# Tile products of a blockwise inverse in two PSUM banks, and other slots for the small work around them, in a gated DeltaNet and S5 decoder step

## The chip, the cores and the metric

One Trainium2 chip, one core. The metric is the device time of one execution of the whole program, in microseconds. In the profile PE is TensorE's matmuls, PEld its weight loads, DVE VectorE, ACT ScalarE, POOL GpSimd, SP the engine that only issues DMAs.

## The reference, cut to what matters

The program is one inference step of a two-layer decoder trunk on 1024 prompt tokens and 8 sample tokens, model width 1024. Layer 0 mixes tokens with a gated DeltaNet, layer 1 with an S5 state-space mixer; each is followed by a SwiGLU FFN. The change touches the DeltaNet mixer alone:

```
qkv, z, b, a = split(h @ w_in);  qkv = silu(short_conv(qkv));  q, k = l2norm(q), l2norm(k)
kb   = k * beta;   decay = exp(gc_i - gc_j) below the diagonal       # gc: running sum of g in a chunk
lmat = tril(kb @ k.T * decay, -1)
w, u = (I + lmat)^-1 @ [kb * exp(gc), v * beta]                      # the inverse, chunk by chunk
per chunk:  v_new = u - w @ S;  o = (q * exp(gc)) @ S + (q @ k.T * decay) @ v_new
            S = S * exp(g_last) + k_dec.T @ v_new
out = (rmsnorm(o) * silu(z)) @ w_out
```

There are 8 query/key heads, each with two value heads. All of it is float32.

## The kernel before, in words

**Staging.** The kernel works on transposed activations, [feature, token], 1032 tokens in three blocks of 344. It goes through a prologue, the mixer, FFN, S5 mixer, GLU and a second FFN. A weight matrix goes through the array as a high and a low part (whi, wlo), so that one product takes three matmuls. POOL makes the two parts of the next weight unit as soon as PE has finished the unit that held the buffer (`split`, L2099 to L2102: a cast, then a subtraction).

**The mixer** loops over 8 head pairs i (`HQK`). A pair has first its dense part: six units of projection (`dense_steps`, L626), with convolution, silu and norms on ACT and DVE. Then come four quads q. A quad is two chunks of 128 tokens of two heads, so four 128 x 128 matrices to invert. The inverse is built by levels: four levels of 32 x 32 tile products along the diagonal (`levels`, `tiles`, L660), a fifth (L762, L767, L773) and a sixth of 64 x 64 (L783, L789). Each level is the same exchange: PE makes the product P of the stored factor (NM) with the inverse so far; ACT copies P out of PSUM (PP, L1020); PE makes the products T and Y from it; DVE adds both to TY (L1282). Nothing of the next level can start before that.

**What fills the waits.** A quad has 12 slots, two to a level, and every engine's program is written out by hand in that order (`slot` in each of `mix_pe`, `mix_act`, `mix_dve`). In a slot stand pieces of other work: steps of the recurrence of the quad before (`chain`, L671, L677, L683 to L690: kS, vn, o, S); pieces of the output projection of the pair before (`out_piece`, L702, six matmuls each, in the slots that `PIECE_SLOTS` names, added into x by `add_x`, L1172); the gate's norm (`gate_sq`, the matmul with ones L638, `gate_r`, `gate_mul` L1085 and L1086, `gate_hi` L883, `gate_lo` L1092); the next quad's Gram product (L653, slot 7) and what DVE makes of it (`triangle` L1124 and L1128 in slot 8, `first_y` L1134 to L1139 in slot 9, which the next quad's first level waits for); the samples' small products (L727, slot 5).

**At a quad's end**, ACT has in slot 9 `spread_t` (two copies, L900), `diagonal` (three copies of the next quad's diagonal blocks, L894), `spread_y` (four copies, L905), and in slot 10 `fifth_y` (two copies, L911) and the copy of VB (L962). DVE has the copy T5 (L1285). PE's sixth level (L783) waits for T5 and Y5; its second product (L789) waits for ACT's copy PP6 (L1022); DVE copies the result to Y (L1288), and the next quad's vn waits for that.

**Banks.** PSUM has eight banks. The tile products of matrix j use bank j (`LEV`, banks 0 to 3), with P, T and Y in separate columns; the recurrence has bank 4. So the fillers of a quad (`aside`) have banks 5, 6 and 7, and take the one that is free first by the slot number given to it. A bank taken again is waited for until its reader is done. The dense part takes seven banks in turn (`take`). The bank of the Gram product is given as free one slot on, while its reader (`triangle`) runs in slot 8.

Of the kernel before, what the change touches and what calls it, by code (L numbers as in the profile page):

```python
# [23 lines left out]
P = 128  # L24
# [29 lines left out]
def build(nc, dr, plan):  # L54
    ctx = ExitStack()
    with ctx:
# [502 lines left out]
        COL_P, COL_T, COL_Y = 0, Z, 2 * Z  # L559
        DENSE = (0, 1, 2, 3, 5, 6, 7)  # L560
        LEV, CB = (0, 1, 2, 3), 4
# [4 lines left out]
        def across(col, w, r=slice(0, P)):  # L566
            return ps[r, 0:4, col:col + w]
        PIECE_SLOTS = ((0, 1, 2, 3, 4, 7, 8, 9), (0, 2, 3, 4, 6, 7), (0, 3, 4, 7, 8), (0, 3, 4, 6, 7))
# [25 lines left out]
        def mix_pe(p):  # L594
            held = {}
            dense = 0
            free = {5: 0, 6: 0, 7: 0}
# [8 lines left out]
            def take(who, name):  # L606
                nonlocal dense
                dense += 1
                return use(DENSE[(dense - 1) % 7], who, name)
# [46 lines left out]
            def tiles(col, lhsT, rhs):  # L656
                for d in range(4):
                    for j in range(4):
                        r = zone((j + d) % 4)
                        ins = nc.tensor.matmul(ps[r, LEV[j], col:col + Z], lhsT(r, j), rhs(r, j), start=True, stop=True)  # L660
                return ins

            def chain(i, q, k):
# [9 lines left out]
                elif k % 4 == 1:  # L673
                    p.after("DVE", g + "Y6")
                    b = use(CB, "ACT", g + f"vn{c}")
# [77 lines left out]
            def fifth_level(i, q):  # L753
# [4 lines left out]
                for j in range(4):  # L758
                    for h in range(2):
                        jj = (j + h) % 4  # L760
                        up, low = zone(2 * h), zone(2 * h + 1)
                        ins = nc.tensor.matmul(ps[low, LEV[jj], COL_P:COL_P + Z], DEC[q % 2][up, jj, low], W[up, jj, 0:Z], start=True, stop=True)  # L762
# [3 lines left out]
                for j in range(4):  # L766
                    ins = nc.tensor.matmul(ps[zone(1), LEV[j], COL_T:COL_T + Z], W[zone(1), j, Z:2 * Z], PP[zone(1), j], start=True, stop=True)  # L767
                p.go(ins, gq + "T5")
                for j in range(4):
                    for h in range(2):  # L770
                        jj = (j + h) % 4
                        up, low = zone(2 * h), zone(2 * h + 1)
                        ins = nc.tensor.matmul(ps[up, LEV[jj], COL_Y:COL_Y + Z], PP[low, jj], W[low, jj, Z:2 * Z], start=True, stop=True)  # L773
                p.go(ins, gq + "PY5")

            def last_level(i, q):
# [3 lines left out]
                p.after("DVE", gq + "T5")  # L780
                p.after("ACT", gq + "Y5")
                for j in range(4):
                    ins = nc.tensor.matmul(ps[H:P, LEV[0], j * H:(j + 1) * H], DEC[q % 2][0:H, j, H:P], TOP[0:H, j], start=True, stop=True)  # L783
# [1451 lines left out]
```

How the kernel before makes its waits and increments, by code:

```python
            def until(self, who, value):  # L126
                if value > self.seen.get(who, 0):
                    self.e.wait_ge(sems[who], value)
                    self.seen[who] = value
# [73 lines left out]
        def wait_weights(p, u):  # L203
            p.e.wait_ge(w_split, place[u] + 1)
            return place[u] % 2
# [124 lines left out]
        def norm_blocks_dve(v, gi, ready=None):  # L330
            V = nc.vector
            for n in range(2):
                for kt in range(KT):
                    if square_by(n, kt) == "DVE":
                        square(v, n, kt, ready)
            v.e.wait_ge(in_par, 16 * 6)
            for k in range(NC3 * KT + 2):
                n, kt = divmod(k, KT)
                if n < NC3:
                    if k >= RING:
                        v.after("DVE", f"lo{(k - RING) // KT}.{(k - RING) % KT}")
                    v.after("ACT", f"rms{n}")
                    v.go(V.scalar_tensor_tensor(ring(nh, k), x[:, kt, blk(n)], gains[:, gi, kt:kt + 1], nr[:, blk(n)], ALU.mult, ALU.mult), f"h{n}.{kt}")
                if k >= 2:
                    n, kt = divmod(k - 2, KT)
                    v.after("ACT", f"hi{n}.{kt}")
                    v.go(V.tensor_tensor(hlo[:, kt, blk(n)], ring(nh, k - 2), hhi[:, kt, blk(n)].bitcast(F32), ALU.subtract), f"lo{n}.{kt}")
# [64 lines left out]
        def pro_pe(p):  # L412
            p.e.wait_ge(const_ready, 1)
            def low_bank(who, name):
                plan[("bank", p.pfx + name)] = int(name[-1])
                return int(name[-1])
```

## Time and profile before

| what | value |
|---|---|
| three runs, median | 3659.48 us (3659.13 to 3660.59) |
| the profiled execution, its own time | 3668.19 us |
| its span, first to last instruction | 3666.5 us |
| busy: PE, PEld, DVE, ACT, POOL | 3337.3, 3143.0, 1865.3, 827.3, 847.5 us |
| granted TensorE clock, mean | 0.922 |
| DMA | 223.82 MB, mean 61 GB/s |

The profiled execution took 8.7 us more than the median run. A granted clock of 1.00 is 2.4 GHz, 0.50 is 1.2 GHz; a mean between them is a mixture of stretches at these two.

### The profile page before, as it was taken

What the parts mean: (1) busy time and instruction counts of PE and PEld (TensorE: products, weight loads), DVE (VectorE), ACT (ScalarE), POOL (GpSimd) and SP (SyncE); (2) the same over time, 40 slices, a digit from 0 to 9 for tenths busy, and PEclk for the clock granted to TensorE, in tenths of its full rate; (3) what the DMA queues carried; (4) which work ended last, traced back from release to release, by engine and by line L of the source; (5) the groups of instructions that cost most, each with busy time, mean ns of one, the idle gap of its engine ahead of it and who ended that gap; (6) DMA issues with size and microseconds to landing.
All of it is one profiled execution on the core that took longest, in us unless ns stands there. A gap on an engine that the chain in (4) does not pass through costs nothing.

```text
span 3666.5 us, 74612 instructions
## 1 busy us (share of the span) xinstructions
PE 3337.3 (91%) x32699; PEld 3143.0 (86%) x32699; DVE 1865.3 (51%) x4027; ACT 827.3 (23%) x1897; POOL 847.5 (23%) x776
## 2 busy tenths in 40 slices
PE   6889898989898898988999999995699899999998
PEld 5878797978787787877999999994499799999997
DVE  5445555455554454556876777635512433423334
ACT  3334333324242332333010111002200300000001
POOL 2102020202020111201333333332323133333331
PEclk8879898989898897989999999996699899999999
DMA  2111111111111111110112222226611011111111
GB/s 90 55 42 50 59 44 59 47 49 52 48 54 44 55 55 49 48 42 30 49 61 84 72 84 78 71 65 217 180 41 47 29 47 47 47 47 47 47 48 62
DMA packets 111348, 223.82 MB, mean 61 GB/s; under 512 B 24880, under 2 KB 59184, under 8 KB 110000
## 3 DMA queue, kind: packets, MB, share of 16 engines
q1 hardware_dynamic: 82400, 177.66, 15.2%
q10 hardware_dynamic: 28624, 41.38, 3.5%
q8 instruction: 259, 4.24, 0.5%
q14 instruction: 65, 0.53, 0.1%
HBM read 177.86 MB, written 41.14 MB: 60 GB/s over the span
## 4 chain that ended last, share of the span: by engine, by line
PE 85%; DVE 8%; ACT 3%; issue 2%; DMA 2%; SPq 1%; POOL 0%; POOLq 0%; DVEq 0%; ACTq 0%
PE ps L218 31%; PE ps L626 15%; PE ps L1360 14%; PE ps L702 5%; PE ps L660 4%; PE ps L677 1%; PE ps L234 1%; PE ps L671 1%; PE ps L653 1%; PE ps L638 1%; DVE x L1172 1%; PE ps L727 1%; PE ps L789 1%; PE ps L295 1%; DVE dwork L1282 1%
## 5 line engine op out<-in xcount | busy, mean ns | idle before, releaser
L218 PE MATMUL ps<-hhi,whi 128*128 128x344 f32 x2424 | 779.1, 321 | 19.1 <-DVE hlo L1829 15.3
L218 PE MATMUL ps<-hhi,wlo 128*128 128x344 f32 x2424 | 776.3, 320 | 0.0
L218 PE MATMUL ps<-hlo,whi 128*128 128x344 f32 x2424 | 775.6, 320 | 0.0
L2099 POOL TENSOR_TENSOR wtick<-wtick 128x1 f32<-128x1 f32 x213 | 46.5, 218 | 2619.4 <-PE ps L218 811.9
L2102 POOL TENSOR_TENSOR wlo<-wraw,whi 128x1024 fp32r<-128x1024 f32 x213 | 531.1, 2493 | 17.1
L218 PEld LDWEIGHTS ps<-hhi,whi 128*128 128x128 f32 x2424 | 457.6, 189 | 21.8 <-issue 17.0
L218 PEld LDWEIGHTS ps<-hhi,wlo 128*128 128x128 f32 x2424 | 457.3, 189 | 0.0
L218 PEld LDWEIGHTS ps<-hlo,whi 128*128 128x128 f32 x2424 | 456.7, 188 | 0.1
L626 PE MATMUL ps<-hhi,whi 128*128 128x344 f32 x1152 | 395.6, 343 | 5.1 <-DVE olo L1092 2.7
L626 PE MATMUL ps<-hhi,wlo 128*128 128x344 f32 x1152 | 376.2, 327 | 0.0
L626 PE MATMUL ps<-hlo,whi 128*128 128x344 f32 x1152 | 376.1, 326 | 0.0
L1469 DVE TENSOR_TENSOR x<-ps,x 128x344 f32<-128x344 f32 x528 | 261.5, 513 | 170.2 <-PE ps L1360 170.2
L1360 PE MATMUL ps<-ahi,wlo 128*128 128x344 f32 x1056 | 338.3, 320 | 0.0
L1360 PE MATMUL ps<-ahi,whi 128*128 128x344 f32 x1056 | 338.1, 320 | 0.1
L1360 PE MATMUL ps<-alo,whi 128*128 128x344 f32 x1056 | 337.5, 320 | 0.0
L1453 DVE TENSOR_TENSOR ab<-ps,sg 128x344 f32<-128x344 f32 x132 | 68.1, 517 | 493.9 <-PE ps L218 486.8
L626 PEld LDWEIGHTS ps<-hhi,whi 128*128 128x128 f32 x1152 | 224.6, 195 | 13.1 <-issue 11.0
L1396 ACT ACTIVATE sg<-ps 128x344 f32<-128x344 f32 x132 | 59.9, 458 | 778.6 <-PE ps L218 767.5
L626 PEld LDWEIGHTS ps<-hlo,whi 128*128 128x128 f32 x1152 | 224.2, 195 | 6.6 <-issue 5.0
L1282 DVE TENSOR_TENSOR dwork<-ps,dwork 128x256 f32<-128x256 f32 x128 | 54.4, 425 | 335.5 <-PE ps L660 335.4
L626 PEld LDWEIGHTS ps<-hhi,wlo 128*128 128x128 f32 x1152 | 223.8, 194 | 0.0
L2100 POOL CAST whi<-wraw 128x1024 fp32r<-128x1024 f32 x213 | 223.3, 1048 | 0.4
(366 smaller groups left out, 5544.1 us busy)
## 6 DMA issues: line engine op xcount, KB each, us to landing
wraw<-in_w SPq DMA_DIRECT2D x213, 512.0 KB, 3.3
dwork<-keep_rows SPq DMA_DIRECT2D x64, 256.0 KB, 3.7
tab<-keep_tab SPq DMA_DIRECT2D x8, 1088.0 KB, 6.4
S<-in_sin ACTq DMA_DIRECT2D x16, 512.0 KB, 3.7
drw<-keep_del SPq DMA_DIRECT2D x32, 256.0 KB, 3.3
out_sout<-S ACTq DMA_DIRECT2D x16, 512.0 KB, 2.8
keep_u<-hs SPq DMA_DIRECT2D x8, 580.0 KB, 3.2
uu<-keep_u SPq DMA_DIRECT2D x8, 580.0 KB, 7.7
```

The lines of the kernel that those rows point to most:

```text
L218: ins = nc.tensor.matmul(out, w, r[:, kt, blk(n)], start=k == 0, stop=k == 3 * KT - 1)
L626: ins = nc.tensor.matmul(ps[:, b, 0:NB], w, r[:, kt, blk(n)], start=k == 0, stop=k == 3 * KT - 1)
L660: ins = nc.tensor.matmul(ps[r, LEV[j], col:col + Z], lhsT(r, j), rhs(r, j), start=True, stop=True)
L702: ins = nc.tensor.matmul(ps[:, b, 0:NB], w[:, s, c:c + P], r[:, kt, blk(n)], start=k == 0, stop=k == 5)
L1282: v.go(V.tensor_tensor(W, across(COL_T, 2 * Z), W, ALU.add), gq + f"TY{l}")
L1360: ins = nc.tensor.matmul(out, w[:, s, c:c + P], r[:, e % 2, kt, blk(n)], start=q == 0, stop=q == 5)
L1396: a.go(nc.scalar.activation(sg[:, j, blk(n)], ps[:, a.bank(f"sg{f}.{j}.{n}"), 0:NB], AF.Silu), f"sg{f}.{j}.{n}")
L1453: v.go(V.tensor_tensor(ab[:, j, blk(n)], ps[:, v.bank(f"ab{f}.{j}.{n}"), 0:NB], sg[:, j, blk(n)], ALU.mult), f"ab{f}.{j}.{n}")
L1469: v.go(V.tensor_tensor(x[:, m, blk(n)], ps[:, v.bank(f"x{e}.{m}.{n}"), 0:NB], x[:, m, blk(n)], ALU.add), f"x{e}.{m}.{n}")
L2099: G.tensor_tensor(wtick[:, 1:2], wtick[:, 0:1], wtick[:, 0:1], ALU.add)
L2100: G.tensor_copy(whi[:, slot, :], wraw[:, slot, :]).then_inc(w_hi, 1)
L2102: G.tensor_tensor(wlo[:, slot, :], wraw[:, slot, :], whi[:, slot, :].bitcast(F32), ALU.subtract).then_inc(w_split, 1)
```

## The change

- P of all four matrices goes to bank 0 and T and Y of all four to bank 1, in adjacent columns, so that ACT and DVE read one contiguous stretch of one bank. The order of the tile products is now matrix by matrix, and the four row and column zones in turn within one.
- The fillers get five banks (2, 3, 5, 6, 7). The dense part enters its banks in that record with the order in which they were taken, and each pair after the first begins its turn at bank 0.
- ACT: T5 is copied by ACT, first in slot 10 (`fifth`), then the two Y5 copies, then two of the `spread_y` copies and VB; the other two `spread_y` copies stand behind the copy PP6. `diagonal` leaves ACT; DVE makes the three copies at the end of `triangle`.
- Gate work in a quad: `gate_mul` from slot 5 to 7, `gate_lo` from 7 to 10, `gate_hi` from 6 to 9 (behind `spread_t`, ahead of `fifth`). Between pairs, the first gate's product with ones stands behind the fourth step of the recurrence, not the first, and `gate_mul` behind its steps 3 and 4.
- The output pieces stand in other slots: of a pair's 24, all four leave slot 7, one slot 8 and one slot 2; slots 5, 6 and 9 get two more each.
- Ahead of its sixth level PE waits for ACT's T5 alone, in place of DVE's T5 and ACT's Y5; vn waits for the `spread_y` copies too.

The diff, with the unchanged lines around it left out for the most part:

```diff
--- before.py
+++ after.py
@@ -556,16 +556,18 @@
         SLOTS = 12
-        COL_P, COL_T, COL_Y = 0, Z, 2 * Z
         DENSE = (0, 1, 2, 3, 5, 6, 7)
-        LEV, CB = (0, 1, 2, 3), 4
+        LP, LT, CB = 0, 1, 4
 
 
-        def across(col, w, r=slice(0, P)):
-            return ps[r, 0:4, col:col + w]
-        PIECE_SLOTS = ((0, 1, 2, 3, 4, 7, 8, 9), (0, 2, 3, 4, 6, 7), (0, 3, 4, 7, 8), (0, 3, 4, 6, 7))
+        def of_p(r=slice(0, P)):
+            return ps[r, LP, 0:4 * Z].rearrange("p (j n) -> p j n", n=Z)
+
+        def of_ty(r=slice(0, P)):
+            return ps[r, LT, 0:8 * Z].rearrange("p (j n) -> p j n", n=2 * Z)
+        PIECE_SLOTS = ((0, 1, 2, 3, 4, 6, 8, 9), (0, 3, 4, 5, 6, 9), (0, 3, 4, 6, 9), (0, 3, 4, 5, 6))
         CHAIN_SLOT = {0: 0, 1: 1, 2: 2, 3: 3, 6: 4, 7: 5, 8: 6, 9: 7}
@@ -593,8 +595,8 @@
             held = {}
-            dense = 0
-            free = {5: 0, 6: 0, 7: 0}
+            dense = base = 0
+            free = {2: 0, 3: 0, 5: 0, 6: 0, 7: 0}
 
@@ -606,7 +608,10 @@
                 dense += 1
-                return use(DENSE[(dense - 1) % 7], who, name)
+                b = DENSE[(dense - 1) % 7]
+                if b in free:
+                    free[b] = base + dense / 100
+                return use(b, who, name)
 
@@ -653,12 +658,21 @@
 
-            def tiles(col, lhsT, rhs):
-                for d in range(4):
-                    for j in range(4):
-                        r = zone((j + d) % 4)
-                        ins = nc.tensor.matmul(ps[r, LEV[j], col:col + Z], lhsT(r, j), rhs(r, j), start=True, stop=True)
+            def tiles(out, lhsT, rhs):
+                for j in range(4):
+                    for z in range(4):
+                        r = zone(z)
+                        ins = nc.tensor.matmul(out(r, j), lhsT(r, j), rhs(r, j), start=True, stop=True)
                 return ins
+
+            def to_p(r, j):
+                return ps[r, LP, Z * j:Z * j + Z]
+
+            def to_t(r, j):
+                return ps[r, LT, 2 * Z * j:2 * Z * j + Z]
+
+            def to_y(r, j):
+                return ps[r, LT, 2 * Z * j + Z:2 * Z * j + 2 * Z]
 
@@ -672,6 +686,7 @@
                     p.after("DVE", g + "Y6")
+                    p.after("ACT", g + "YD")
                     b = use(CB, "ACT", g + f"vn{c}")
@@ -757,30 +772,26 @@
                     for h in range(2):
-                        jj = (j + h) % 4
                         up, low = zone(2 * h), zone(2 * h + 1)
-                        ins = nc.tensor.matmul(ps[low, LEV[jj], COL_P:COL_P + Z], DEC[q % 2][up, jj, low], W[up, jj, 0:Z], start=True, stop=True)
+                        ins = nc.tensor.matmul(to_p(low, j), DEC[q % 2][up, j, low], W[up, j, 0:Z], start=True, stop=True)
                 p.go(ins, gq + "P5")
                 for j in range(4):
-                    ins = nc.tensor.matmul(ps[zone(1), LEV[j], COL_T:COL_T + Z], W[zone(1), j, Z:2 * Z], PP[zone(1), j], start=True, stop=True)
-                p.go(ins, gq + "T5")
+                    ins = nc.tensor.matmul(to_t(zone(1), j), W[zone(1), j, Z:2 * Z], PP[zone(1), j], start=True, stop=True)
                 for j in range(4):
                     for h in range(2):
-                        jj = (j + h) % 4
                         up, low = zone(2 * h), zone(2 * h + 1)
-                        ins = nc.tensor.matmul(ps[up, LEV[jj], COL_Y:COL_Y + Z], PP[low, jj], W[low, jj, Z:2 * Z], start=True, stop=True)
+                        ins = nc.tensor.matmul(to_y(up, j), PP[low, j], W[low, j, Z:2 * Z], start=True, stop=True)
                 p.go(ins, gq + "PY5")
                 slot(i, q, 10)
-                p.after("DVE", gq + "T5")
-                p.after("ACT", gq + "Y5")
+                p.after("ACT", gq + "T5")
                 for j in range(4):
-                    ins = nc.tensor.matmul(ps[H:P, LEV[0], j * H:(j + 1) * H], DEC[q % 2][0:H, j, H:P], TOP[0:H, j], start=True, stop=True)
+                    ins = nc.tensor.matmul(ps[H:P, LP, j * H:(j + 1) * H], DEC[q % 2][0:H, j, H:P], TOP[0:H, j], start=True, stop=True)
                 p.go(ins, gq + "P6")
@@ -797,20 +808,21 @@
                     p.after("DVE", gq + f"TY{l - 1}")
-                    p.go(tiles(COL_P, lambda r, j: NM[r, l - 1, j], lambda r, j: W[r, j, 0:Z]), gq + f"P{l}")
+                    p.go(tiles(to_p, lambda r, j: NM[r, l - 1, j], lambda r, j: W[r, j, 0:Z]), gq + f"P{l}")
                     slot(i, q, 2 * (l - 1) + 1)
                     p.after("ACT", gq + f"P{l}")
-                    tiles(COL_T, lambda r, j: W[r, j, Z:2 * Z], lambda r, j: PP[r, j])
-                    p.go(tiles(COL_Y, lambda r, j: PP[r, j], lambda r, j: W[r, j, Z:2 * Z]), gq + f"PY{l}")
+                    tiles(to_t, lambda r, j: W[r, j, Z:2 * Z], lambda r, j: PP[r, j])
+                    p.go(tiles(to_y, lambda r, j: PP[r, j], lambda r, j: W[r, j, Z:2 * Z]), gq + f"PY{l}")
                 fifth_level(i, q)
                 e = i - 1
+                dense, base = (0 if i else 2), i * NQ * SLOTS - 1
                 for k, _ in enumerate(dense_steps(i, 0)):
                         chain(e, NQ - 1, k)
-                        if k == 0:
+                        if k == 3:
                             gate(f"{e}.{NQ - 2}.", QCH * CH)
@@ -826,14 +838,15 @@
                 gram(i, 0, take)
+                free[DENSE[(dense - 1) % 7]] = base + 2
                 for _ in dense_steps(i, 5):
                     pass
-                for b in LEV:
+                for b in (LP, LT):
                     p.after(*held[b])
                     levels(i, q)
-                for b in LEV:
-                    held[b] = ("ACT", f"{i}.{NQ - 1}.P6")
+                held[LP] = ("ACT", f"{i}.{NQ - 1}.P6")
+                held[LT] = ("ACT", f"{i}.{NQ - 1}.Y5")
             e = HQK - 1
@@ -887,28 +900,22 @@
 
-            def diagonal(i, q):
-                g = f"{i}.{q}."
-                a.after("DVE", g + "NT")
-                for z in range(1, 4):
-                    a.go(A.activation(DEC[q % 2][zone(z), :, 0:Z], DEC[q % 2][zone(z), :, zone(z)], AF.Copy), g + "NTc")
-
             def spread_t(i, q):
 
-            def spread_y(i, q):
-                g = f"{i}.{q}."
-                for z in range(4):
-                    a.go(A.activation(YY[q % 2][zone(z), :, zone(z)], TY[q % 2][zone(z), :, Z:2 * Z], AF.Copy), g + "YD")
-
-            def fifth_y(i, q):
+            def spread_y(i, q, zones):
+                for z in zones:
+                    a.go(A.activation(YY[q % 2][zone(z), :, zone(z)], TY[q % 2][zone(z), :, Z:2 * Z], AF.Copy), f"{i}.{q}.YD")
+
+            def fifth(i, q):
                 g = f"{i}.{q}."
                 a.after("PE", g + "PY5")
-                for z in (0, 2):
-                    a.go(A.activation(YY[q % 2][zone(z), :, zone(z + 1)], across(COL_Y, Z, zone(z)), AF.Copy), g + "Y5")
+                a.go(A.activation(TOP[zone(1), :, 0:Z], of_ty(zone(1))[:, :, 0:Z], AF.Copy), g + "T5")
+                for z in (2, 0):
+                    a.go(A.activation(YY[q % 2][zone(z), :, zone(z + 1)], of_ty(zone(z))[:, :, Z:2 * Z], AF.Copy), g + "Y5")
 
@@ -937,8 +944,6 @@
                     decay(i, q + 1)
-                if s == 6 and q >= 2:
-                    gate_hi(f"{i}.{q - 2}.", gate_cols(q - 2), f"{i - 1}.out{KT - 1}.{q - 2}" if i else None)
                 if q == NQ - 1:
@@ -953,11 +958,11 @@
                     spread_t(i, q)
-                    if q + 1 < NQ:
-                        diagonal(i, q + 1)
-                    spread_y(i, q)
+                    if q >= 2:
+                        gate_hi(f"{i}.{q - 2}.", gate_cols(q - 2), f"{i - 1}.out{KT - 1}.{q - 2}" if i else None)
                 if s == 10:
-                    fifth_y(i, q)
+                    fifth(i, q)
+                    spread_y(i, q, (2, 3))
                     a.after("PE", g + "vT")
@@ -975,8 +980,10 @@
                 if i:
+                    for k in (1, 2):
+                        chain(e, NQ - 1, k)
                     gate_r(f"{e}.{NQ - 2}.", QCH * CH)
-                    for k in (1, 2, 5, 6):
+                    for k in (5, 6):
                         chain(e, NQ - 1, k)
@@ -1006,8 +1013,6 @@
                         a.go(A.activation(zb[:, t, blk(n)], ps[:, a.bank(g + f"z{t}.{n}"), 0:NB], AF.Silu), g + f"z{t}.{n}")
-                        if t == 1 and n == 0:
-                            diagonal(i, 0)
                 A.preload_act_table_set(LOGEXP)
@@ -1017,9 +1022,10 @@
                                 a.after("PE", gq + f"PY{l - 1}")
-                            a.go(A.activation(PP, across(COL_P, Z), AF.Copy), gq + f"P{l}")
+                            a.go(A.activation(PP, of_p(), AF.Copy), gq + f"P{l}")
                         else:
-                            a.go(A.activation(PP6[H:P], ps[H:P, LEV[0], 0:4 * H].rearrange("p (j n) -> p j n", n=H), AF.Copy), gq + "P6")
+                            a.go(A.activation(PP6[H:P], ps[H:P, LP, 0:4 * H].rearrange("p (j n) -> p j n", n=H), AF.Copy), gq + "P6")
+                            spread_y(i, q, (0, 1))
                         slot(i, q, 2 * (l - 1) + 1)
@@ -1126,11 +1132,14 @@
                     v.go(V.scalar_tensor_tensor(M[:, j], ps[:, b, (2 + j % 2) * P:(3 + j % 2) * P], tg[:, 0, j // 2, c:c + 1], M[:, j], ALU.mult, ALU.mult), g + "NT")
+                v.after("DVE", g + "NT")
+                for z in range(1, 4):
+                    v.go(V.tensor_copy(M[zone(z), :, 0:Z], M[zone(z), :, zone(z)]), g + "NTc")
 
                 W, M = TY[q % 2], DEC[q % 2]
-                v.after("ACT", g + "NTc")
+                v.after("DVE", g + "NTc")
                 v.go(V.tensor_tensor(W[:, :, Z:2 * Z], M[:, :, 0:Z], lev[:, 0].unsqueeze(1).to_broadcast([P, 4, Z]), ALU.mult), g + "Y0a")
@@ -1194,9 +1203,9 @@
                         gate_sq(i, q - 2)
-                    if s == 5:
+                    if s == 7:
                         gate_mul(i, q - 2)
-                    if s == 7:
+                    if s == 10:
                         gate_lo(i, q - 2)
@@ -1249,9 +1258,10 @@
                     gate_sq(e, NQ - 2)
+                    for k in (3, 4):
+                        chain(e, NQ - 1, k)
                     gate_mul(e, NQ - 2)
-                    for k in (3, 4, 7):
-                        chain(e, NQ - 1, k)
+                    chain(e, NQ - 1, 7)
                 tables(i)
@@ -1279,11 +1289,8 @@
                             v.after("PE", gq + f"PY{l}")
-                            v.go(V.tensor_tensor(W, across(COL_T, 2 * Z), W, ALU.add), gq + f"TY{l}")
-                        elif l == 5:
-                            v.after("PE", gq + "T5")
-                            v.go(V.tensor_copy(TOP[zone(1), :, 0:Z], across(COL_T, Z, zone(1))), gq + "T5")
-                        else:
+                            v.go(V.tensor_tensor(W, of_ty(), W, ALU.add), gq + f"TY{l}")
+                        elif l == 6:
                             v.after("PE", gq + "PY6")
```

## Rows read from the trace of the kernel before

**Rows 1.** The page's chain that ended last, by engine

```profile
PE 85%; DVE 8%; ACT 3%; issue 2%; DMA 2%; SPq 1%; POOL 0%; POOLq 0%; DVEq 0%; ACTq 0%
```

**Rows 2.** Windows, mixer and rest: length, busy per engine, TensorE clock, DMA share, GB/s

```profile
71.00:1670.00 1599.00, 1434.20 (x20881) 1294.30 (x20880) 821.12 (x2036) 542.39 (x1311) 236.35 (x192) 0.88 0.16 50
1670.00:3666.50 1996.50, 1865.36 (x11680) 1821.08 (x11680) 1002.21 (x1912) 258.60 (x530) 589.88 (x536) 0.96 0.22 69
```

**Rows 3.** Groups of PE instructions by form: busy, mean ns | idle before, releasers

```profile
L660 PE MATMUL ps<-dwork 32*32 32x32 f32 x12288 | 168.5, 201 | 18.8 <-DVE dwork L1282 8.1 <-issue 5.3 <-ACT dwork L1020 4.6
L702 PE MATMUL ps<-ohi,whi 128*128 128x344 f32 x384 | 152.4, 397 | 37.2 <-DVE dwork L1128 19.2 <-DVE x L1172 14.6 <-ACT zb L1008 3.3
...
L638 PE MATMUL ps<-gsq,ones 128*128 128x512 f32 x64 | 39.9, 710 | 17.0 <-DVE gsq L1079 17.0
L783 PE MATMUL ps<-dwork 64*64 64x64 f32 x256 | 29.1, 277 | 55.0 <-ACT yinv L911 26.0 <-DVE S L1167 17.0 <-ACT dwork L911 8.4
L677 PE MATMUL ps<-dwork 128*128 128x128 f32 x128 | 28.1, 352 | 6.9 <-DVE dwork L1163 6.8
L677 PE MATMUL ps<-dwork,yinv 128*128 128x128 f32 x128 | 26.9, 345 | 11.3 <-DVE dwork L1163 11.3
```

**Rows 4.** Timeline of ACT at the end of the second quad, sixth head pair

```profile
1165.95 0.62 ACT L900 ACTIVATE dwork<-dwork 32x128 f32<-32x128 f32 x2
1167.54 0.97 ACT L894 ACTIVATE dwork<-dwork 32x128 f32<-32x128 f32 x3 [0.97 <-DVE dwork L1128]
1168.53 1.30 ACT L905 ACTIVATE yinv<-dwork 32x128 f32<-32x128 f32 x4
1169.86 0.56 ACT L911 ACTIVATE yinv<-ps 32x128 f32<-32x128 f32 x2
1170.44 0.60 ACT L962 ACTIVATE dwork<-ps 128x512 f32<-128x512 f32 x1
```

**Rows 5.** Timeline of PE, third and first quad of the same pair, and a full-clock product

```profile
1122.12 0.39 PE L702 MATMUL ps<-ohi,whi 128*128 128x344 f32 x1 [1.13 <-DVE x L1172]
...
1160.56 0.71 PE L677 MATMUL ps<-dwork 128*128 128x128 f32 x4
...
1190.27 1.22 PE L677 MATMUL ps<-dwork,yinv 128*128 128x128 f32 x4 [1.60 <-DVE dwork L1163]
...
1199.12 0.39 PE L702 MATMUL ps<-ohi,whi 128*128 128x344 f32 x1 [2.47 <-DVE dwork L1128]
```

**Rows 6.** Timeline of DVE in the third quad, around slots 5 and 6

```profile
1188.10 0.74 DVE L1085 SCALAR_TENSOR_TENSOR qkv<-qkv,ng,gsq 128x512 f32<-128x512 f32 x1
1188.88 0.69 DVE L1086 TENSOR_TENSOR qkv<-qkv,zb 128x512 f32<-128x512 f32 x1
1189.61 0.61 DVE L1163 SCALAR_TENSOR_TENSOR dwork<-ps,tg,dwork 128x128 f32<-128x128 f32 x2
```

**Rows 7.** Windows of the same pair: columns as in Rows 2

```profile
1163.70:1170.53 6.83, 3.60 (x71) 2.93 (x70) 5.26 (x16) 3.92 (x14) 0.00 (x0) 1.00 0.18 41
1170.53:1177.36 6.83, 6.80 (x63) 5.83 (x64) 2.39 (x7) 1.17 (x3) 0.00 (x0) 0.50 0.11 38
...
1196.04:1212.35 16.31, 11.76 (x188) 9.64 (x186) 8.94 (x28) 5.76 (x19) 2.27 (x3) 0.79 0.24 66
```

**Rows 8.** Groups of DVE copies in the mixer, by form

```profile
L1285 DVE COPY dwork<-ps 32x128 f32<-32x128 f32 x32 | 9.1, 283 | 38.1 <-PE ps L767 37.6
...
L1069 DVE COPY cso<-cst 128x16 f32<-128x16 f32 x32 | 5.2, 164 | 0.0
```

**Rows 9.** Timelines of DVE and POOL in the fourth quad, same stretch

```profile
1226.10 2.77 DVE L1092 TENSOR_TENSOR olo<-qkv,ohi 128x512 fp32r<-128x512 f32 x1
...
1225.97 2.35 POOL L2102 TENSOR_TENSOR wlo<-wraw,whi 128x1024 fp32r<-128x1024 f32 x1
```

**Rows 10.** Timeline of PE: tile products and a single-tile product at full clock

```profile
1142.60 0.65 PE L783 MATMUL ps<-dwork 64*64 64x64 f32 x8 [1.19 <-ACT dwork L911]
...
1154.33 0.76 PE L660 MATMUL ps<-dwork 32*32 32x32 f32 x64
```

## Prediction

> **What bounds the kernel now.** Look at the chain that ended last first: PE carries 85% of it and DVE 8% [rows 1], so time goes down only where PE waits less or runs faster. Then split the span by stage. The change touches the mixer alone, 1599.0 us, and leaves the other 1996.5 us after it as they are. In the mixer PE is busy 1434.2 us, so idle for 165 us, and its granted clock is 0.88 [rows 2]. A clock of 0.88 made of 1.00 and 0.50 means that 0.24 of the mixer, some 384 us, ran at 1.2 GHz. These are the two stores from which the change can draw: 165 us of waits, and what the low clock costs.
>
> **Which waits.** The groups of PE instructions by form show them, with what ended each [rows 3]: 55.0 us ahead of the sixth level (L783), 37.2 us ahead of the output pieces (L702), 18.2 us ahead of vn and L677's two forms (6.9 and 11.3), 18.8 us ahead of the tile products (L660), 17.0 us ahead of the gate's product (L638). That is 146 of the 165 us, and the change touches each of them.
>
> **The change part by part.**
>
> *1. The end of a quad.* The 55.0 us are 1.7 us in each of 32 quads. Read ACT's timeline: two copies 0.62, three diagonal copies 0.97, four spread copies 1.30, and only then the two Y5 copies (0.56) that PE wants, and VB 0.60 [rows 4]. After the change, ACT is free when the fifth level's products end, T5 needs one copy of about 0.3 us, and PE has four transposes of its own meanwhile: this wait goes. But the next becomes late: PE's second product waits for PP6, which now stands behind T5 0.3, Y5 0.56, two spread copies 0.65, VB 0.60 and takes 0.38 itself, 2.5 us in sum (estimate, from rows 4 and the 0.3 of a small copy; PP6 taken between the 0.28 of a Y5 copy and VB's 0.60). PE has L783's products against it (29.1 us busy in 32 quads [rows 3], 0.9 each) and two groups of transposes, some 1.6 us in sum (estimate), so 0.9 us stay in each quad, 29 us in 32. Net: 26 us less; bounds 10 less (ACT late on its entry) and 45 less.
>
> *2. Five filler banks and the pieces' slots.* Of the 37.2 us, 19.2 wait for the reader of the Gram product and 14.6 for the add of an earlier piece [rows 3]. Both are waits for a bank, not for data: one in the first quad's slot 2 is 1.13 us, one in the third quad's slot 8 is 2.47 us, both ended by DVE [rows 5]. With five banks the piece takes another one, and in the third quad it also leaves slot 8. I take 31 of 33.8 us, bounds 15 (the inverse's own exchange is then waited for) and 34. Pieces in slots 5 and 6 also cover part of the 18.8 us ahead of the tile products: 5 us, bounds 0 and 10.
>
> *3. Gate work later.* vn in the third quad waited 1.60 us for X [rows 5]; on DVE, X (L1163) stood behind gate_mul's 0.74 and 0.69 us in slot 5 [rows 6]. Moved to slot 7 it is behind X. I take 14 of the 18.2 us, bounds 8 and 18. The gate's product between pairs waited 17.0 us; behind the fourth step it finds gate_sq long done: 13 us less, bounds 8 and 17.
>
> *4. What this work meets instead.* Take the third quad's turn, from its last TY add to the first one of the fourth quad: 16.3 us, in which DVE is busy 8.9 us and PE 11.8, at a clock of 0.79 [rows 7]. The change brings gate_mul, 1.4 us [rows 6], and the three new copies into this stretch, and takes T5 out. The new copies are not in the trace of before; a 32 x 128 copy from PSUM takes 0.283 us and the shortest copies of SBUF 0.164 [rows 8], so 0.5 to 0.85 us for three, and I take 0.6, nearer the small copies since the source is SBUF. DVE has then 8.9 + 1.4 + 0.6 - 0.3 = 10.6 us, some 11 with the gaps. PE's 11.8 us, of which 6.8 were at the low clock, are 9.0 at the high one (by part 5's price), and 9.9 with the wait of part 1. So DVE is 1 us late at this turn. In the other turns gate_mul is missing, and the 0.3 us more that DVE has there are hidden behind PE. There is more: gate_lo took 2.77 us where POOL was making a weight unit's low part, 2.35 us, at the same time [rows 9]; an operation of that size is 0.69 us otherwise [rows 6]. A unit's buffer comes free with the first piece of the fourth quad, and DVE, now late, has its scaled q and gate_sq in that stretch: nothing to 2.3 us more, I take 1.3. So 2.3 us at 7 turns: 16 us more. In the fourth quad gate_hi stands in ACT's queue ahead of T5 and waits for gate_mul, which runs beside POOL (the last piece is now in slot 6): 1.2 us at 7 quads, 8 us more. Bounds of the two together: 5 and 40 more.
>
> *5. The low clock.* Where it falls: in the stretch 1163.7 to 1170.5, PE is busy 3.60 of 6.83 us, and the next 6.83 us are granted 0.50 [rows 7]. What a stretch costs: the same four matmuls take 1.22 us at the low clock and 0.71 us at the high one [rows 5], so a dense 6.8 us gives back some 2.8 us. The mixer has 384 us at the low clock, near six such stretches in a pair. After parts 1 to 3, the ends of the first and second quad have a piece or transposes where a wait was, and the samples' product in the first quad is followed by a piece. The end of the fourth quad and the third's turn still have waits of over a microsecond. I take a third of the low time as regained: 128 us x 0.41 = 52 us less, taken as 50. Bounds: nothing, and four fifths of it, 125 us.
>
> *6. Reads and order.* PP and TY are read as one contiguous stretch instead of four. The number of elements stays, so I take no change. The tile products in one bank: 64 of them take 0.76 us [rows 10], an order of a matrix's four zones in turn keeps four zones in flight, and I take 0.
>
> **The sum.** 26 + 31 + 5 + 14 + 13 = 89 us less, 24 more, so 65; with the clock 115. The profiled execution took 3668.2 us, 8.7 more than the median of the runs: 3668.2 - 115 = 3553, and on the scale of the medians **3545**. This likeliest case runs from 3510 to 3570.
>
> **The rivals.**
>
> *The clock does not come back* (0.20). Stalls of 0.9 us at each quad's end and the samples' product stay, and the clock falls at the same places. Against it: the fall came after a stretch that was half idle. Then 3660 - 65 = 3595.
>
> *DVE becomes the bound at the turns* (0.15). The delays of part 4 come in more quads than the third, or POOL takes its full 2.3 us each time, and these waits drag the clock. Parts 1 to 3 less 60 us leave 29, and the clock gives 10: 3620.
>
> *The clock comes back nearly everywhere* (0.12). 65 + 125 = 190 us: 3470. For it: 384 us are in store, and the falls all stand at the waits that are removed. Against: the samples' products are untouched.
>
> *The tile products no longer run beside each other* (0.08), which makes it slower. The kernel before gives each matrix its own bank, and no row shows tile products of different zones in the same bank at once. The price: eight 64-column products of a single tile take 0.65 us, 81 ns each, so some 41 ns for 32 columns; now 64 of them take 0.76 us, 12 ns each [rows 10]. One after the other, 12288 of them [rows 3] would cost 29 ns more each, 356 us, all of it on the chain: 3545 + 356 = 3901, or 3723 if half of it. It decides from 21 ns each on, where it eats the 115 us. Against it: a zone's products write the same 32 partitions as before, and no two zones share one; hence the low chance. The Trainium skill (TensorEngine Tiling (Array Packing), Restrictions and Gotchas) says that different row tiles cannot access the same PSUM bank simultaneously, which speaks against the new layout. Its PSUM page (PSUM — Partial Sum Buffer, PSUM bank collisions) narrows the rule to one bank and one 32-partition quadrant, and by that nothing would change. No run of the kernel before shows either.
>
> *The change moves nothing* (0.03): a piece that no longer waits for its bank only lengthens the wait for the next add, and PP6 takes over all of L783's wait. 3655.
>
> **How the numbers follow.** The likeliest case has 0.42. About 0.2%, 7 us, is what a measurement of this kernel can tell from no change. Faster by more: 0.42 + 0.20 + 0.15 + 0.12 = 0.89. Within: 0.03. Slower: 0.08. The range leaves out the slow rival, the one that moves nothing, and the outer halves of the two cases at the ends, and reaches from 3475 to 3615.
>
> **What would show it.** *Right:* the wait ahead of L783 under 10 us in sum and a new one of about 0.9 us ahead of L789; none of the 2.47 us waits at L702; L638 without its 1.97 us; DVE-ended waits in the turn to the fourth quad; mixer clock about 0.92; mixer near 1490 us and the rest at 1996 us. *Wrong:* tile products at over 21 ns each; a mixer clock still at 0.88, or 0.96 and above; waits on DVE's add in every quad. If ACT's contiguous read of PP were shorter than the 0.28 us of before, part 6 would be wrong as well.

## The result and the profile after

The changed kernel takes 3503.66 us (median of four runs, 3502.26 to 3511.36) against 3660.03 us for the kernel before on the same chip: a ratio of 0.9573, 95% interval 0.9553 to 0.9592. It is 156 us faster, 41 more than the forecast's 115, inside the range and just outside the likeliest case's own (3510 to 3570). One execution of all the runs, the profiled one of e12 (3682.56 us at a granted clock of 0.82), took 213 us more than the median of its fellows and is left out of every number here.

The page's chain by engine, and the windows of the mixer and of the rest (columns as in rows 2); they answer to [rows 1, 2]:

```profile
PE 87%; DVE 6%; ACT 3%; issue 2%; DMA 2%; SPq 0%; POOL 0%; POOLq 0%; DVEq 0%; ACTq 0%
...
71.00:1510.00 1439.00, 1358.67 (x20882) 1231.23 (x20881) 841.31 (x2099) 523.13 (x1246) 239.51 (x192) 0.94 0.17 56
1510.00:3503.00 1993.00, 1858.52 (x11680) 1815.62 (x11680) 1004.86 (x1913) 259.46 (x531) 593.32 (x536) 0.96 0.22 69
```

The mixer is 160 us shorter and the rest some 4 us, with unchanged work. In the mixer PE's idle time fell from 165 to 80 us and its busy time, for the same matmuls, from 1434.2 to 1358.7 us. The second number is the clock: 0.88 became 0.94, and the time at the low clock, summed over the clock record of each trace up to the last output piece, fell from 380 to 181 us. So the gain is half waits (84 us) and half clock (76 us).

The groups of PE instructions by form, which answer to [rows 3] (L665 was L660, L717 L702, L643 L638, L794 L783, L692 L677):

```profile
L665 PE MATMUL ps<-dwork 32*32 32x32 f32 x12288 | 162.9, 199 | 7.9 <-DVE dwork L1292 3.6 <-ACT dwork L1025 2.6 <-issue 1.7
L717 PE MATMUL ps<-ohi,whi 128*128 128x344 f32 x384 | 147.6, 384 | 0.0
...
L698 PE MATMUL ps<-dwork,S 128*128 128x128 f32 x256 | 55.6, 300 | 9.3 <-DVE dwork L1154 7.1
...
L643 PE MATMUL ps<-gsq,ones 128*128 128x512 f32 x64 | 34.3, 619 | 3.1 <-DVE gsq L1085 3.1
...
L692 PE MATMUL ps<-dwork 128*128 128x128 f32 x128 | 25.0, 323 | 7.5 <-DVE dwork L1172 7.5
L692 PE MATMUL ps<-dwork,yinv 128*128 128x128 f32 x128 | 24.8, 323 | 0.5 <-DVE dwork L1172 0.5
L794 PE MATMUL ps<-dwork 64*64 64x64 f32 x256 | 22.0, 227 | 6.3 <-ACT dwork L916 6.2
...
L800 PE MATMUL ps<-dwork 64*64 64x64 f32 x128 | 11.8, 238 | 16.3 <-ACT dwork L1027 16.3
L800 PE MATMUL ps<-yinv,dwork 64*64 64x64 f32 x128 | 11.8, 237 | 18.4 <-ACT dwork L1027 18.4
```

The 55.0 us ahead of the sixth level are 6.3; in their place stand 34.7 us ahead of its second product (L800), all ended by ACT's copy PP6. The 37.2 us ahead of the output pieces are gone. The tile products, all in one bank at a time now, take 199 ns on average, as against 201: they still run beside each other (12288 of them are 162.9 us busy, 13 ns each). A plain float32 matmul stands in the profile as two records; so these are 6144 matmuls.

ACT's timeline at the end of the third quad of the sixth pair, and PE's beside it, show the new wait (they answer to [rows 4]):

```profile
1093.31 0.27 ACT L916 ACTIVATE dwork<-ps 32x128 f32<-32x128 f32 x1 [0.76 <-PE ps L785]
1093.60 0.56 ACT L918 ACTIVATE dwork<-ps 32x128 f32<-32x128 f32 x2
1094.19 0.64 ACT L911 ACTIVATE dwork<-dwork 32x128 f32<-32x128 f32 x2
1094.85 0.60 ACT L967 ACTIVATE dwork<-ps 128x512 f32<-128x512 f32 x1
1095.47 0.38 ACT L1027 ACTIVATE dwork<-ps 64x256 f32<-64x256 f32 x1
```

```profile
1093.78 0.68 PE L794 MATMUL ps<-dwork 64*64 64x64 f32 x8
1094.39 0.44 PE L762 MATMUL ps<-ident,qkv 128*128 128x128 f32 x2
1095.90 0.68 PE L800 MATMUL ps<-dwork 64*64 64x64 f32 x8 [1.07 <-ACT dwork L1027]
```

T5 to PP6 is 2.54 us without a gap. PE starts its sixth level as soon as its transposes are issued, but is then idle for 1.07 us, since VB (0.60) and one of the two Y5 copies (the one of zone 0; the second product reads only the other) stand ahead of PP6, and nobody awaits them yet.

### The profile page after: what moved, and what is told of

It reads as the page before. It is cut to its first block, busy times and chain, and to the rows that moved or that the text cites. A ratio compares the mean times of both kernels' runs of the same rounds, so it can differ in the third digit from the quotient of the medians.

```text
span 3503.3 us, 74520 instructions
## 1 busy us (share of the span) xinstructions
PE 3254.5 (93%) x32699; PEld 3073.9 (88%) x32699; DVE 1887.6 (54%) x4091; ACT 808.9 (23%) x1833; POOL 854.3 (24%) x776
## 4 chain that ended last, share of the span: by engine, by line
PE 87%; DVE 6%; ACT 3%; issue 2%; DMA 2%; SPq 0%; POOL 0%; POOLq 0%; DVEq 0%; ACTq 0%
PE ps L218 33%; PE ps L631 16%; PE ps L1367 14%; PE ps L717 5%; PE ps L665 4%; PE ps L234 1%; PE ps L685 1%; PE ps L692 1%; PE ps L658 1%; PE ps L643 1%; PE ps L742 1%; PE ps L295 1%; PE ps L698 1%; DMA uu<-keep_u 1%; PE ps L705 1%
```

## The experiments

Each run was timed in three rounds with the kernel before on the same chip. The last three columns are from the profiled execution, from 71 us to the last output piece: PE's busy time, its idle time (length less busy) and the granted clock.

| kernel | ratio to before (95%) | PE busy | PE idle | clock |
|---|---|---|---|---|
| before | 1 | 1434.2 | 162.5 | 0.88 |
| changed | 0.9573 (0.9553 to 0.9592) | 1358.7 | 78.8 | 0.94 |
| e1 banks only | 0.9922 (0.9904 to 0.9941) | 1426.0 | 136.9 | 0.89 |
| e2 copies only | 0.9915 (0.9892 to 0.9939) | 1424.6 | 139.6 | 0.89 |
| e3 pieces and gate only | 0.9759 (0.9739 to 0.978) | 1394.9 | 112.5 | 0.92 |
| e8 pieces only | 0.9787 (0.9771 to 0.9803) | 1397.3 | 116.6 | 0.92 |
| e9 gate only | 0.9979 (0.9969 to 0.9988) | 1426.9 | 153.6 | 0.89 |
| e4 changed, three filler banks | 0.9588 (0.9568 to 0.9607) | 1366.3 | 73.1 | 0.93 |
| e5 before, idle work | 0.9881 (0.9867 to 0.9896) | 1419.4 | 131.0 | 0.93 |
| e6 changed, idle work | 0.9485 (0.947 to 0.9499) | 1345.5 | 57.8 | 0.98 |
| e7 changed, late VB | 0.9477 (0.946 to 0.9494) | 1345.5 | 60.6 | 0.95 |
| e10 e7, late gate_hi | 0.9441 (0.9417 to 0.9465) | 1337.1 | 47.7 | 0.96 |
| e11 e10, two idle matmuls | 0.9465 (0.9451 to 0.948) | 1343.7 | 55.4 | 0.96 |
| e12 e10, four idle matmuls | 0.9474 (0.9457 to 0.949) | | | |

No trace of e12 is read.

### The parts one at a time

**e1, the banks alone.** The kernel before with `LP, LT`, the new `tiles` and `free = {2: 0, 3: 0, 5: 0, 6: 0, 7: 0}`; copies, gate and pieces as before.

> The kernel before with the bank layout alone: P in bank 0, T and Y in bank 1, five filler banks; copies and slots as before. My theory: the waits of the output pieces (37 us ahead of the piece's matmuls) fall under 8 us, the 55 us ahead of the sixth level stay within 10 us, the 18 us ahead of vn stay; 30 us of waits less and some 15 us of clock: 3660 - 45 = 3615, between 3600 and 3635. Rival (the tile products lose their overlap in one bank): over 3700, 64 of them well over the 0.76 us. Rival (the banks moved nothing): 3660 within 5.

Measured 3635.13 us, 28 less, at the slow edge of what was expected. The waits of the pieces are gone, as expected, but the other waits did not stay as they were, and the groups of PE by form show it:

```profile
L692 PE MATMUL ps<-dwork,yinv 128*128 128x128 f32 x128 | 30.1, 376 | 14.5 <-DVE dwork L1177 14.5
L796 PE MATMUL ps<-dwork 64*64 64x64 f32 x256 | 27.4, 265 | 72.6 <-ACT yinv L925 27.7 <-DVE S L1181 25.1 <-ACT dwork L925 19.7
L692 PE MATMUL ps<-dwork 128*128 128x128 f32 x128 | 27.4, 345 | 9.1 <-DVE dwork L1177 9.0
```

The sixth level now waits 72.6 us instead of 55.0, and vn 23.6 instead of 18.2 [rows 3]. Of the 37.2 us freed at the pieces, 23 came back: PE ran earlier into the next wait, which is for data. The rival with serial tile products falls: they take 201 ns as before.

**e2, the copies alone.** T5 on ACT, the diagonal copies on DVE, the spread copies behind; all banks as before. Here PE has to wait for both Y5 copies, not for T5 alone:

```diff
-                p.after("DVE", gq + "T5")
                 p.after("ACT", gq + "Y5")
```

since the sixth level writes bank 0, which with the old layout the Y5 copies still read. That is the one thing that the two banks do for the copies: P and the pair T, Y no longer share one.

> The kernel before with the copies alone: T5 on ACT, diagonal copies on DVE, spread copies and the wait on them behind; four banks and three filler banks as before, so PE has to wait for the Y5 copies too before its sixth level writes into bank 0. Theory: the wait ahead of the sixth level falls from 55 to some 20 us, one of some 30 us comes ahead of its second product; the clock's falls at the quads' ends get shorter: 3660 - 5 to 10 of waits - 30 of clock = 3620, between 3595 and 3645. Rival (clock does not react): 3650.

Measured 3631.95 us, 31 less (0.9915). The sixth level's wait fell from 55.0 to 21 us, 14 us came ahead of its second product (30 were expected), and the clock hardly moved (0.89): PE's busy time fell by 10 us, not by the 30 expected.

**e3, pieces and gate together, e8 and e9, each alone.** The edits are those lines of the change. The one of e8 is this one line:

```diff
-        PIECE_SLOTS = ((0, 1, 2, 3, 4, 7, 8, 9), (0, 2, 3, 4, 6, 7), (0, 3, 4, 7, 8), (0, 3, 4, 6, 7))
+        PIECE_SLOTS = ((0, 1, 2, 3, 4, 6, 8, 9), (0, 3, 4, 5, 6, 9), (0, 3, 4, 6, 9), (0, 3, 4, 5, 6))
```

> The kernel before with the moved slots alone: gate work and output pieces as in the changed kernel, banks and copies as before. Theory: 14 us ahead of vn and 13 us ahead of the gate's product go; with three filler banks the pieces still wait, 15 to 35 us; gate_hi ahead of the copies at the quad's end costs 0.6 us in 16 quads, 10 us: 3660 - 20 - 15 of clock = 3625, between 3605 and 3650. Rival (the slots make the gain): under 3560.

> The kernel before with the output pieces' slots alone. In the run with all moved slots the time fell by 88 us with the banks as before. Theory (the pieces' places carry it: they keep PE busy where it would wait for the inverse's exchange or for a reader, and the clock falls less): 3660 - 60 = 3600, between 3585 and 3625. Rival (the gate's places carry it): 3640 or more.

> The kernel before with the moved gate work alone, pieces, banks and copies as before. Pieces alone gave 0.9787, pieces and gate work together 0.9759. Theory: 14 us ahead of vn and 13 us ahead of the gate's product go, but gate_hi ahead of the copies at the quad's end lengthens the wait ahead of the sixth level by 10 to 15 us: 3660 - 10 = 3650, between 3635 and 3660. Rival (the two add up and pieces were helped by nothing): 3645 or less.

Measured 3575.28, 3587.02 and 3654.83 us: 0.9759, 0.9787 and 0.9979. One line of constants is worth half of the whole change, and more than banks and copies together. e3 beat its own expectation (3605 to 3650): the pieces wait 14.1 us there, not 15 to 35, and PE's busy time fell by 39 us, not by 15. The groups of e8, with three filler banks as before:

```profile
L660 PE MATMUL ps<-dwork 32*32 32x32 f32 x12288 | 166.6, 200 | 6.9 <-DVE dwork L1282 3.7 <-ACT dwork L1020 1.7 <-ACT zb L1008 0.9
L702 PE MATMUL ps<-ohi,whi 128*128 128x344 f32 x384 | 150.8, 393 | 14.1 <-DVE x L1172 10.8 <-ACT zb L1008 3.3
...
L677 PE MATMUL ps<-dwork 128*128 128x128 f32 x128 | 26.7, 339 | 3.9 <-DVE dwork L1163 3.8
L677 PE MATMUL ps<-dwork,yinv 128*128 128x128 f32 x128 | 25.4, 330 | 3.1 <-DVE dwork L1163 3.1
L783 PE MATMUL ps<-dwork 64*64 64x64 f32 x256 | 22.9, 235 | 55.0 <-ACT yinv L911 24.0 <-ACT dwork L911 17.7 <-DVE dwork L1139 10.5
```

The waits for the Gram product's reader are gone (19.2 us), vn waits 7.0 instead of 18.2 us although gate_mul still stands ahead of X, because a piece in slot 6 now lies between the product that X reads and vn, and the tile products wait 6.9 instead of 18.8 us. The sixth level waits the same 55.0 us, so here the waits did not move on: the pieces fill places, ahead of vn and among the tile products, at which PE would wait in any case. And of the 83 us by which its mixer is shorter, 37 are PE's busy time: the clock.

Of e9, two rows show why moving gate work gains next to nothing by itself:

```profile
L702 PE MATMUL ps<-ohi,whi 128*128 128x344 f32 x384 | 151.5, 394 | 43.3 <-DVE dwork L1130 25.2 <-DVE x L1174 14.8 <-ACT zb L1010 3.3
...
L783 PE MATMUL ps<-dwork 64*64 64x64 f32 x256 | 29.2, 277 | 74.8 <-DVE olo L1094 25.4 <-ACT yinv L911 24.7 <-ACT dwork L911 12.4
```

vn's wait and the gate's fell to 3.1 us each, but triangle stands behind gate_mul now (43.3 for 37.2 us) and the sixth level behind gate_lo (25.4 of its 74.8 us, in the fourth quads; it was 55.0 in all).

**e4, the extra banks taken back.** The changed kernel with `free = {5: 0, 6: 0, 7: 0}`.

> The changed kernel with the fillers on banks 5, 6 and 7 again, all else as changed. Theory: the pieces wait again for a bank, 15 to 30 us, and the clock takes 10 to 20 us more: 3504 + 35 = 3539, between 3520 and 3560. Rival (with the pieces in other slots the two extra banks are not needed): 3504 within 7.

Measured 3510.21 us, 0.9588 against 0.9573, with intervals that overlap: outside what was expected, and within the rival's 7 us. Whether the two banks still bring a few microseconds is not settled; that they bring 20 or more is excluded. With the pieces in their new slots a filler seldom meets a bank that is held.

### The clock

**e5 and e6, idle work.** Extra float32 matmuls with results that nothing reads, at the end of each quad: in the kernel before five, ahead of the wait for the sixth level, in the changed one four, ahead of the wait for its second product. They go to a filler bank that is free by then:

```diff
+            def idle_work(n):
+                b = min(free, key=lambda k: (free[k], k))
+                if b in held:
+                    p.after(*held.pop(b))
+                for _ in range(n):
+                    nc.tensor.matmul(ps[:, b, 0:P], ident[:, :], ones[:, :], start=True, stop=True)
...
                 slot(i, q, 10)
+                idle_work(5)
                 p.after("DVE", gq + "T5")
                 p.after("ACT", gq + "Y5")
```

> The kernel before with five extra 128 x 128 float32 matmuls at the end of each quad, ahead of PE's wait for the sixth level; their results are not used. They fit into the wait (1.7 us a quad) and take none away. Theory (the wait drags the clock down): the mixer's clock rises from 0.88 to 0.91 and the time falls by 20 to 50 us: 3625. Rival (only the waits count, or the falls come from elsewhere): no change or up to 10 us more.

> The changed kernel with four such matmuls at the end of each quad, ahead of PE's wait for the second product of the sixth level (1.08 us each). Theory: some of the low stretches left stand behind quads' ends: 3504 - 15, between 3480 and 3500. Rival (they come from the samples' product and the start of the quads): 3504 to 3510.

Measured 3619.83 us for e5, 44 less than before, and 3474.72 us for e6, 29 less than the changed kernel, with more work in each. The windows of their mixers:

```profile
71.00:1621.40 1550.40, 1419.35 (x21201) 1289.00 (x21200) 825.29 (x2033) 540.55 (x1309) 238.09 (x189) 0.93 0.16 52
```

```profile
71.00:1474.30 1403.30, 1345.46 (x21136) 1224.67 (x21136) 840.86 (x2097) 521.92 (x1245) 235.73 (x189) 0.98 0.18 57
```

In e5 the clock is 0.93 for 0.88, and PE is busy 15 us less although the 160 matmuls more (320 records) make some 46 us of it:

```profile
L616 PE MATMUL ps<-ones,ident 128*128 128x128 f32 x320 | 46.0, 295 | 0.5 <-DVE x L1180 0.5
```

The pieces and the gate's product wait as before (37.4 and 17.0 us), vn 21.9 for 18.2 us. The wait ahead of the sixth level is 23.2 for 55.0 us because it is filled; it is not saved. So the gain is the clock's: the low clock does hang, in part, on the waits at the quads' ends, in both kernels, and the rival by which it would not react falls. In the changed kernel the time at the low clock fell from 181 to 78 us with the idle work: more than half of what was left hung on the wait for PP6. The time, 3474.72 us, is below what was expected (3480 to 3500).

### A faster version

**e7.** VB and the Y5 copy of zone 0 move on ACT behind PP6 (`fifth_y` makes the Y5 copy of one zone):

```diff
-                for z in (2, 0):
-                    a.go(A.activation(YY[q % 2][zone(z), :, zone(z + 1)], of_ty(zone(z))[:, :, Z:2 * Z], AF.Copy), g + "Y5")
+                fifth_y(i, q, 2)
...
                     spread_y(i, q, (2, 3))
-                    a.after("PE", g + "vT")
-                    a.go(A.activation(f4(VB), ps[:, a.bank(g + "vb"), :], AF.Copy), g + "vb")
...
+                            a.after("PE", gq + "vT")
+                            a.go(A.activation(f4(VB), ps[:, a.bank(gq + "vb"), :], AF.Copy), gq + "vb")
+                            fifth_y(i, q, 0)
                             spread_y(i, q, (0, 1))
```

> The changed kernel with VB and one Y5 copy moved on ACT behind the copy PP6 that PE waits for. Theory: the wait of 1.08 us ahead of the second product falls to about 0.2 us in each of 32 quads, 27 us, and the clock gives 5 to 15 more: 3504 - 35 = 3469, between 3455 and 3485. Rival (VB comes too late for X on DVE and for vn, which then wait): 3495 to 3510.

Measured 3469.71 us, 34 less than the changed kernel: 6.1 us are left of the 34.7 (waits of PE, L800), and 8.8 us came ahead of the next quad's first kS, which waits for DVE's S. The profiled execution took 3481.04 us, 11 more than the median.

**e10.** In the fourth quad gate_hi leaves its place ahead of T5 too, and gate_lo follows it into slot 11.

> The run with late VB, and in the fourth quad gate_hi behind PP6 and gate_lo one slot later. Theory: the 5.4 us ahead of the sixth level in the fourth quads go: 3470 - 8 = 3462, between 3452 and 3472. Rival (gate_lo then delays DVE's Y6 and vn): 3470 or more.

Measured 3455.35 us, ratio 0.9441: the lowest median of the study, 48 us under the changed kernel and 204 under the one before. Against e7 it is 14 us, on another chip, and the two intervals just touch. The wait ahead of the sixth level is gone. Its largest waits of PE in the mixer:

```profile
PE ps L685 <- DVE S L1180: 8.7, 10, 1.3
PE ps L692 <- DVE dwork L1176: 7.6, 11, 1.1
PE ps L643 <- DVE gsq L1089: 6.5, 10, 3.5
PE ps L800 <- ACT dwork L1028: 5.3, 31, 0.3
```

ACT is no longer ahead of the list; DVE is.

**e11 and e12, idle work on top.**

> The same with two unused 128 x 128 float32 matmuls ahead of the second product of the sixth level, where 0.2 us of wait are left. They cost some 0.45 us in each of 32 quads, 8 us net, and can only win by the clock, of whose low stretches 139 us are left. Theory: a third of them go, 18 us: 3462 - 10 = 3452, between 3440 and 3465. Rival (the falls left are not at the quads' ends): 3470.

> The same with four: 0.9 us a quad, 22 us net of the wait, against up to two thirds of the low time, 37 us. Theory: 3450 to 3465, no better than with two. Rival (clock does not react): 3484.

Measured 3466.84 and 3469.61 us (the second a median of three runs): ratios 0.9465 and 0.9474 against e10's 0.9441, with intervals that overlap; no gain is to be had and a loss is likely. Where no wait is left to put them in, the matmuls cost more than the clock gives (0.96 in both e10 and e11): PE is busy 6.6 us more in e11 and idle 7.7 us more. Both expectations, 3452 and 3450 to 3465, were missed.

## Why the prediction was right, and where not

**The frame was right.** Two stores, waits and clock; the mixer alone; faster by over a hundred. Predicted 65 us of waits and 50 of clock, measured 84 and 76. In the waits the pieces and the tile products gave 6 us more each than their terms and vn 3 more, the turn to the fourth quad and the fourth quad's end cost 2 less each, and against that the end of a quad gave 6 us less.

**Part 1, the end of a quad: right, slightly mis-sized.** The sixth level's wait went in the first three quads, and PP6's took its place, 1.08 us in each quad for the 0.9 named: 34.7 us for 29. ACT's 2.5 us from T5 to PP6 are 2.54; PE's work against it is shorter.

**Part 2, the banks: the waits went, the value of the banks was wrong.** The step said that both waits are "for a bank, not for data", and that five banks remove 31 of 33.8 us. So far as it goes that holds: banks alone free all 37.2 us at the pieces. But 23 come back at the next waits for data (e1); the pieces' places alone remove 23 of the 37 with the old banks, and nothing comes back (e8); without the extra banks the changed kernel loses nothing clear (e4). The lower bound of 15 us, "the inverse's own exchange is then waited for", was the right value for the banks. What the step left out is the value of a piece's place, which I priced at 5 us for the tile products' waits; they fell by 11 us, and the clock came with them.

**Part 3, gate work later: each wait went, the gain was not its own.** The gate's product waits 3.1 us for 17.0. vn's waits stood in slot 7 of the third and fourth quads, behind gate_mul as the step says (11.3 and 6.6 us); less than 1 us of them is left. The 8.0 us that vn still waits are for the most part new, in slot 1 of the fourth quad, and belong to part 4: 17 us went for the 14 taken. But the gate's slots alone give 0.2% (e9), and vn's wait falls as far with the pieces alone. Banks 28, copies 31 and both kinds of slots 88 us make 147 of the 156 in sum, so these three nearly add up; pieces and gate are 77 and 5 alone and 88 together.

**Part 4, the turn to the fourth quad: right.** DVE's 11 us over the turn are 11.5 in the sixth pair, 10.50 of them busy, as the window shows (columns as in rows 2; it answers to the last of [rows 7]):

```profile
1090.07:1101.61 11.54, 10.09 (x187) 8.24 (x186) 10.50 (x32) 5.74 (x18) 2.49 (x2) 0.85 0.28 88
```

In the fourth quads 14 us of waits end with DVE, for the 16 named: 6.8 ahead of the first vn and 7.1 ahead of o. The 7.1 are the meeting with POOL that the step expected: in five of the seven turns the scaled q (L1154) took 2.90 to 3.02 us for 0.74, beside POOL's subtraction, and PE waited 1.4 to 1.5 us for it; in the other two, the sixth pair's among them, it waited 0.22 us at most. In the seventh pair:

```profile
1273.19 3.02 DVE L1154 TENSOR_TENSOR dwork<-dwork,qkv 128x256 f32<-128x256 f32 x2
...
1273.53 2.40 POOL L2109 TENSOR_TENSOR wlo<-wraw,whi 128x1024 fp32r<-128x1024 f32 x1
...
1276.27 0.49 PE L698 MATMUL ps<-dwork,S 128*128 128x128 f32 x2 [1.49 <-DVE dwork L1154]
```

The three new copies take 0.72 us at the turns, for the 0.6 taken. The fourth quad's end waits 6.3 us for 8, by the mechanism named: in the sixth pair gate_mul's first operation took 1.72 us instead of 0.74, beside POOL's subtraction.

```profile
1114.37 1.72 DVE L1091 SCALAR_TENSOR_TENSOR qkv<-qkv,ng,gsq 128x512 f32<-128x512 f32 x1
```

```profile
1113.18 2.36 POOL L2109 TENSOR_TENSOR wlo<-wraw,whi 128x1024 fp32r<-128x1024 f32 x1
```

**Part 5, the clock: mechanism right, size too small.** This is the term that carries most of the miss: the low time fell by more than half (380 us to 181), not by a third, and PE's busy time by 76 us, not 50. The price was right: 76 us for 199 us of low time are 0.38 each, for the 0.41 taken. I took the low stretches as six a pair (384 us make seven of 6.83 us) that go or stay. There were 55 in the mixer, 6.9 us in the mean; 38 are left, and they became shorter, 4.8 us. The pieces' places alone took the low time to 263 us (e8), the idle work at the quads' ends to 239 (e5). In the kernel before the one shown lasts 6.83 us [rows 7]; of the changed one, behind the end of the fourth quad, these windows show the fall and the rise:

```profile
1114.34:1121.17 6.83, 4.55 (x72) 3.55 (x71) 4.41 (x9) 4.90 (x15) 1.20 (x1) 1.00 0.23 71
1121.17:1124.58 3.41, 3.41 (x15) 3.41 (x14) 0.90 (x4) 0.00 (x0) 0.00 (x0) 0.50 0.83 308
1124.58:1131.40 6.82, 6.82 (x49) 6.82 (x49) 1.88 (x5) 1.01 (x3) 0.00 (x0) 1.00 0.02 8
```

PE was busy without a gap in the low stretch there, and the clock was back after 3.41 us.

**Part 6, reads and order: right.** PP's copy is 0.28 us as before and the tile products 199 ns for 201.

Of the rivals, that the clock does not come back fell (0.94, and e5 and e6), and so did the one that it comes back nearly everywhere, though it went further than the likeliest case. DVE became a bound at the turns to the fourth quad only, and the change did move the time. The tile products run beside each other in one bank, so the slow rival fell too. The Trainium skill's rule that different row tiles cannot access one bank at the same time (TensorEngine Tiling (Array Packing), Restrictions and Gotchas) thus does not hold here, where each zone writes 32 partitions of its own; the Trainium skill's PSUM page (PSUM — Partial Sum Buffer, PSUM bank collisions) states that collision of row tiles for one bank and one 32-partition quadrant, and with that the trace agrees (199 ns for 201).

## What to carry to other kernels

A wait whose releaser is the reader of a buffer is worth only what the next wait for data leaves of it (14 of 37 us here): try the piece of work in another place of the order before more buffers are spent. When PE waits in short, regular gaps, price the gaps twice, once as idle time and once by the clock of what follows; a few unused matmuls in the gap measure the second price by themselves. On an engine that serves an awaited copy, look at what stands ahead of it that nobody awaits yet.

## What was not expected of the hardware

- Matmuls with no use made the kernel 44 us faster (e5) and the changed one 29 us (e6), by the granted clock (0.88 to 0.93, 0.94 to 0.98).
- DVE and POOL seem to hold each other up, now the one, now the other. In five of the seven turns to the fourth quad DVE's scaled q was the slow one (part 4). In the other two POOL's cast took 2.52 and 2.55 us, for 1.03 to 1.11, and DVE's scaled q, begun 0.3 us behind it, its usual 0.74. This is read from the timing, not tried by itself. In the sixth pair:

```profile
1099.25 2.52 POOL L2107 CAST whi<-wraw 128x1024 fp32r<-128x1024 f32 x1
...
1099.52 0.74 DVE L1154 TENSOR_TENSOR dwork<-dwork,qkv 128x256 f32<-128x256 f32 x2
...
1112.07 1.04 POOL L2107 CAST whi<-wraw 128x1024 fp32r<-128x1024 f32 x1
```

- Three float32 copies of 32 x 128 within SBUF took 0.72 us on DVE (the shortest 0.22 us each, for 0.283 out of PSUM [rows 8]). In the eight dense parts they took 1.5 to 1.8 us, as here beside POOL's subtraction; that is why the mean of the group is 0.287:

```profile
L1137 DVE COPY dwork<-dwork 32x128 f32<-32x128 f32 x96 | 27.6, 287 | 3.1
...
136.74 2.40 POOL L2109 TENSOR_TENSOR wlo<-wraw,whi 128x1024 fp32r<-128x1024 f32 x1
...
138.22 1.50 DVE L1137 COPY dwork<-dwork 32x128 f32<-32x128 f32 x3
...
1093.87 0.72 DVE L1137 COPY dwork<-dwork 32x128 f32<-32x128 f32 x3
```
